# Expert jobs of 96 rows in place of 128 in a two-layer hybrid model kernel

## What is computed

```python
def swiglu(h, w1, w3, w2):
    return (jax.nn.silu(h @ w1) * (h @ w3)) @ w2

def moe_swiglu(h, w_router, w1, w3, w2):
    logits = (h @ w_router).astype(jnp.float32)
    top_v, top_i = lax.top_k(logits, TOP_K)            # TOP_K = 2
    gates = jax.nn.softmax(top_v, axis=-1)
    ...
    for e in range(N_EXPERTS):                          # 8
        out = out + combine[..., e:e + 1] * swiglu(h, w1[e], w3[e], w2[e])
```

## Time and profile before

| what | value |
|---|---|
| runs | 1646.36, 1650.67 and 1651.36 us, median 1650.67 |
| span of the profiled execution | 1645.5 us |
| PE busy | 1585.1 us, 96% of the span |
| DVE busy, ACT busy | 1283.7 us, 1041.8 us |
| expert part | from 672.4 us to 1634.4 us of the span |
| weights of the expert part | 336 loads of 1 MB |

### The profile page before, as it was taken

One profiled execution on the slowest core, in us unless ns is written; L12 is line 12 of the kernel. 1 busy time (PEld: TensorE's weight loads), 2 busy tenths in 40 slices (PEclk: granted clock), 3 DMA queues, 4 the chain that ended last, 5 costly groups with the idle time before them and its releaser, 6 DMA issues.

```text
span 1645.5 us, 27766 instructions
## 1 busy us (share of the span) xinstructions
PE 1585.1 (96%) x10290; PEld 1363.3 (83%) x10290; DVE 1283.7 (78%) x1252; ACT 1041.8 (63%) x1038; POOL 139.9 (9%) x152
## 2 busy tenths in 40 slices
PE   7999989999899999899999999999999999999997
PEld 7987789999898778788888888888888888888776
DVE  4885556555558656688889889889888888988997
ACT  4634454344354445577777777777777777777675
POOL 1062000000006200100000000000000000001720
PEclk9999999999999999999999999999999999999999
DMA  7429165542252105699999999999999999999992
GB/s 252 159 89 398 55 256 184 186 170 99 80 176 88 40 2 225 247 374 375 382 375 374 389 375 377 382 374 384 378 375 361 399 373 367 395 373 369 398 356 111
DMA packets 68272, 457.56 MB, mean 278 GB/s; under 512 B 7296, under 2 KB 8480, under 8 KB 16752
## 3 DMA queue, kind: packets, MB, share of 16 engines
q1 hardware_dynamic: 59984, 425.80, 67.1%
q0 software_dynamic: 8080, 30.84, 4.9%
q10 hardware_dynamic: 144, 0.05, 0.0%
HBM read 433.07 MB, written 23.59 MB: 278 GB/s over the span
## 4 chain that ended last, share of the span: by engine, by line
PE 54%; issue 3%; DVE 3%; ACT 2%; DVEq 0%; ACTq 0%
PE bank L417 33%; PE bank L442 17%; DVE wl L495 2%; PE bank L430 1%; ACT wh L491 1%; PE bank L738 1%; PE bank L1271 1%; DVE gl L586 0%; PE bank L814 0%; PE bank L1276 0%; PE bank L483 0%; DVE gate L577 0%; ACT wide L1770 0%; ACT oh L728 0%; DVE rstd L2026 0%
## 5 line engine op out<-in xcount | busy, mean ns | idle before, releaser
L495 DVE TENSOR_TENSOR wl<-ring,wh 128x2048 fp32r<-128x2048 f32 x369 | 854.0, 2318 | 157.7 <-ACT wh L491 154.4
L491 ACT ACTIVATE wh<-ring 128x2048 fp32r<-128x2048 f32 x369 | 706.6, 1917 | 99.5 <-PE bank L442 46.9
L417 PE MATMUL bank<-wh,xh 128*128 128x512 f32 x896 | 358.0, 400 | 3.6 <-DVE wl L495 3.0
L417 PE MATMUL bank<-wh,xl 128*128 128x512 f32 x896 | 350.3, 391 | 0.0
L417 PE MATMUL bank<-wl,xh 128*128 128x512 f32 x896 | 349.6, 390 | 0.0
L417 PEld LDWEIGHTS bank<-wh,xh 128*128 128x128 f32 x896 | 168.3, 188 | 36.7 <-DVE wl L495 3.7
L417 PEld LDWEIGHTS bank<-wh,xl 128*128 128x128 f32 x896 | 168.2, 188 | 35.5
L417 PEld LDWEIGHTS bank<-wl,xh 128*128 128x128 f32 x896 | 168.7, 188 | 32.2
L442 PE MATMUL bank<-wh,gh 128*128 128x512 f32 x448 | 175.4, 392 | 6.3 <-DVE gl L586 6.3
L442 PE MATMUL bank<-wh,gl 128*128 128x512 f32 x448 | 174.4, 389 | 0.0
L442 PE MATMUL bank<-wl,gh 128*128 128x512 f32 x448 | 174.3, 389 | 0.0
(11 more groups left out here) (336 smaller groups left out, 2434.2 us busy)
## 6 DMA issues: line engine op xcount, KB each, us to landing
ring<-in_moe_w SPq DMA_DIRECT2D x336, 1024.0 KB, 5.0
ring<-in_ffn_w SPq DMA_DIRECT2D x33, 1024.0 KB, 4.8
ring<-in_w_in SPq DMA_DIRECT2D x24, 1024.0 KB, 4.9
ring<-in_w_out SPq DMA_DIRECT2D x8, 1024.0 KB, 4.8
job_x<-xrow POOLq DMA_DIRECT2D x1, 8192.0 KB, 27.3
job_y<-xrow POOLq DMA_DIRECT2D x1, 8192.0 KB, 47.7
xrow<-job_x POOLq DMA_DIRECT2D x7, 512.0 KB, 9.3
job_y<-yj POOLq DMA_DIRECT2D x7, 512.0 KB, 4.4
```

Of the source, the lines that this page charges most:

```text
L417: ins = nc.tensor.matmul(up_bank(run, par, 0)[:], x[:, 0:C], w[b][:, k], **kw)
L491: nc.scalar.activation(wh[:, buf], flat_slot(slot), ACT.Copy).then_inc(sem("w_high"), 1)
L495: nc.vector.tensor_tensor(wl[:, buf], flat_slot(run.place(i)[0]), wh[:, buf].bitcast(F32), ALU.subtract).then_inc(sem("w_split"), 1)
```

## The change

`C` becomes 96. Every place where C and the number of partitions P were the same number is told apart: tiles that hold one row of a job in each partition use 96 partitions, matmuls whose stationary operand is the job's rows have 96 stationary columns, and matmuls and transposes whose output's free dimension is the rows have 96 columns. The buffers in DRAM have 16 x 96 rows. The comparison that counts an expert's jobs is made for b = 1 and b = 2 where it was made for b = 1. No instruction of a loop is added, removed or moved on any engine. The core of the diff:

```diff
-C = P
+C = 96
                             if run.moe:
-                                ins = nc.tensor.matmul(up_bank(run, par, 0)[:], x[:, 0:C], w[b][:, k], **kw)
+                                ins = nc.tensor.matmul(up_bank(run, par, 0)[0:C], x[:, 0:C], w[b][:, k], **kw)
                 for a in range(2):
-                    ins = nc.tensor.transpose(bank[TURNS][:, a * P:(a + 1) * P], gate[:, 0, a * P:(a + 1) * P], cst("id"))
+                    ins = nc.tensor.transpose(bank[TURNS][:, a * C:(a + 1) * C], gate[0:C, 0, a * P:(a + 1) * P],
+                                              cst("id")[0:C, 0:C])
                         if run.moe:
-                            ins = nc.tensor.matmul(bank[2 + o][:], g[:, a, 0:C], w[b][:, a, o * 512:(o + 1) * 512],
+                            ins = nc.tensor.matmul(bank[2 + o][0:C], g[:, a, 0:C], w[b][:, a, o * 512:(o + 1) * 512],
-                nc.scalar.activation(silu[:, item], up_bank(run, par, item)[:, 0:T], ACT.Silu, bias=cst("zero")
+                nc.scalar.activation(silu[0:C, item], up_bank(run, par, item)[0:C, 0:T], ACT.Silu, bias=cst("zero", C)
-                nc.vector.tensor_tensor(gate[:, item], up_bank(run, par, item)[:, T:2 * T], silu[:, item], ALU.mult
+                nc.vector.tensor_tensor(gate[0:C, item], up_bank(run, par, item)[0:C, T:2 * T], silu[0:C, item], ALU.mult
-                        turn(bank[5 + half][:, d * C:(d + 1) * C], xrow[:, k * P:(k + 1) * P],
-                             sig="gathered" if d == 3 else None)
+                        turn(bank[5 + half][:, d * C:(d + 1) * C], xrow[0:C, k * P:(k + 1) * P], C,
+                             "gathered" if d == 3 else None)
-                    nc.vector.tensor_tensor(xl[:, hv, 0:C], bank[5 + half][:].rearrange("p (k c) -> p k c", c=C),
+                    nc.vector.tensor_tensor(xl[:, hv, 0:C], bank[5 + half][:, 0:4 * C].rearrange("p (k c) -> p k c", c=C),
-                pool.dma_start(xrow[:], job_x[bass.ds(j * C, C), :]).then_inc(sem("x_loaded"), 16)
+                pool.dma_start(xrow[0:C], job_x[bass.ds(j * C, C), :]).then_inc(sem("x_loaded"), 16)
```

More of the change, by code:

```diff
@@ L792, in yrow, with placed @@
             return (xT, wide)[tt][:].rearrange("p (a b) t -> p a (b t)", a=2)[:, i]
-        def placed(tt=slice(0, TT)):
-            return gh[:, tt, C:2 * C]
+        def placed(tt):
+            return gh[0:C, tt, P:2 * P]
         def y_part(low, half):
-            return (xh, xl)[low][:, 4 * half:4 * half + 4, C:2 * C]
+            return (xh, xl)[low][0:C, 4 * half:4 * half + 4, P:2 * P]
         def acc_half(half):
-            return bank[2 + half][:].rearrange("p (k c) -> p k c", c=C)
+            return bank[2 + half][0:C].rearrange("p (k c) -> p k c", c=P)
         LAST_BANKS = ((5, 6), (0, 1))
@@ L881, in pe_moe @@
             for tt in range(TT):
-                turn(bank[7][:, tt * P:(tt + 1) * P], sel[:, tt], sig="place_turned" if tt else None)
+                turn(bank[7][0:C, tt * P:(tt + 1) * P], sel[:, tt], sig="place_turned" if tt else None)
             pe_down(pe, run, last, True)
@@ L904, in gathered @@
                     nc.scalar.activation(xh[:, 4 * half:4 * half + 4, 0:C],
-                                         bank[5 + half][:].rearrange("p (k c) -> p k c", c=C), ACT.Copy
+                                         bank[5 + half][:, 0:4 * C].rearrange("p (k c) -> p k c", c=C), ACT.Copy
                                          ).then_inc(sem("x_high"), 1)
@@ L911, in acc @@
                 for half in range(2):
-                    nc.scalar.copy(yj[:, half * 512:(half + 1) * 512], bank[2 + half][:]).then_inc(sem("acc_copied"), 1)
+                    nc.scalar.copy(yj[0:C, half * 512:(half + 1) * 512], bank[2 + half][0:C]).then_inc(sem("acc_copied"), 1)
             last = PAIRS_E - 1
@@ L935, in act_moe @@
             act.wait_ge(sem("place_turned"), 1)
-            nc.scalar.activation(placed(), bank[7][:, 0:T].rearrange("p (a c) -> p a c", c=C), ACT.Copy).then_inc(sem("last_high"), 1)
+            nc.scalar.activation(gh[0:C, :, P:2 * P], bank[7][0:C, 0:T].rearrange("p (a c) -> p a c", c=P), ACT.Copy).then_inc(sem("last_high"), 1)
             f(tiny[:], cst("zero"), ACT.Sqrt)
@@ L1003, in dve_moe @@
             for i in range(2):
-                settle(nc.vector.tensor_tensor(hit[:, i], cst("iota").unsqueeze(1).broadcast_to([P, TT, C]),
+                settle(nc.vector.tensor_tensor(hit[:, i], cst("iota")[:, 0:C].unsqueeze(1).broadcast_to([P, TT, C]),
                                                choice("slot")[:, i].unsqueeze(2).broadcast_to([P, TT, C]), ALU.is_equal))
@@ L1077, in load @@
             def load(j):
-                pool.dma_start(xrow[:], job_x[bass.ds(j * C, C), :]).then_inc(sem("x_loaded"), 16)
+                pool.dma_start(xrow[0:C], job_x[bass.ds(j * C, C), :]).then_inc(sem("x_loaded"), 16)
             def store(j):
                 pool.wait_ge(sem("acc_copied"), 2 * j + 2)
-                pool.dma_start(job_y[bass.ds(j * C, C), :], yj[:]).then_inc(sem("y_stored"), 16)
+                pool.dma_start(job_y[bass.ds(j * C, C), :], yj[0:C]).then_inc(sem("y_stored"), 16)
             pool.dma_start(fin, A["final_norm"].rearrange("(a d) -> a d", a=1).broadcast_to([P, D])
@@ L1253, in _ @@
                         pool.dma_start(rows_.rearrange("(j p) d -> p j d", p=C),
-                                       xrow[:].unsqueeze(1).broadcast_to([P, MAXJOBS, D])).then_inc(sem(sig), 16)
+                                       xrow[0:C].unsqueeze(1).broadcast_to([C, MAXJOBS, D])).then_inc(sem(sig), 16)
                 settle(nc.gpsimd.memset(xft[H:P, :, 0:H], 0.0))
```

## The result

The change took 1657.11 us, the median of 6 runs (1650.28 to 1658.58), against 1647.51 us, the median of 6 runs of the kernel before (the three known ahead and three more). The ratio is 1.0044 with a 95% interval of 1.0028 to 1.006: a little slower, clear of the noise, where 1644.4 us had been forecast. (The ratios here are not quotients of the medians. The profiled execution took 1650.28 us with a span of 1648.7, 3.2 us over the span of before.

The account below looks back on a forecast made before the run. PE's pace was taken to bound the expert part, most of the time. Transposes 4.8, hand-over 0.9 and start and end 0.6 summed to 6.3 us off 1650.67, giving 1644.4 us, range 1630 to 1652.

Parts of the forecast that it names:

- The 4032 large matmuls: Expert matmuls streaming 512 columns past the narrowed operand: starts stay 227 ns apart, loads hidden; 0 us, at most 13 less.
- Number of jobs: Router result: no expert has more than 78 rows, so eight jobs stay eight; a ninth would cost 119 us.
- Transposes: 4.8 us: Two PE transposes a pair move 96 columns instead of 128: 50 ns less in 12 pairs of each of 8 jobs.
- Hand-over: 0.9 us: DVE between jobs: two shorter `gl`, 67 ns less each, over 7 hand-overs.
- Start and end: 0.6 us: Shorter operations before job 0's first down projection and at the end, between 0 and 0.8 us less.
- Costed at nothing: Row loads, `yj` stores and zero fills become a quarter smaller but are covered, so 0 us.
- 1 (transposes keep their time): Transposes bound by the 128-column load or a fixed cost: 1.5 us gain remains, 1649.2 us, no change; chance 0.17.
- 2 (the 13 ns shrink: The rest in the large matmuls' 227 ns shrinks with width: 19 us less in total, 1631 us; chance 0.10.
- 3 (a drain at each switch of shape: Switching between 96 and 128 rows empties PE around the transposes: 32 us more, 1676 us; chance 0.08.
- 4: The router gives nine jobs instead of eight: 1763 us; chance 0.01.
- 5: Weight loads of the large matmuls are exposed after all: 26 ns each, 105 us less, 1540 us; chance 0.01.

Follow-up runs that it names:

- run 2: The kernel before with only the large matmuls' stationary operand narrowed to 96 columns; 1658.14 us, ratio 1.0061.
- run 5: The changed kernel itself measured again, unaltered, over 12 runs; 1653.44 us, ratio 1.002.
- run 1: The changed kernel with the large matmuls' stationary operand 128 columns wide again, columns 96 to 127 zeroed on DVE; 1650.66 us, ratio 1.002.
- run 11: The kernel before with the stationary weights of layer 0's dense up projection narrowed from 128 to 96 columns, 256 streamed; 1643.1 us, one run.
- run 12: The changed kernel with 128-wide stationary operands, zero fills from 128 partitions, and columns 96 to 127 zeroed at DVE's expert start, off the routing chain; 1643.70 us, ratio 0.9964.
- 8: The changed kernel with its two DRAM buffers at their old size of 2048 rows; 1656.36 us, ratio 1.0044.
- 10: The changed kernel with the zero fills of the 1536 rows made from 128 partitions; 1651.68 us, ratio 1.002.

## Why the prediction was wrong, by its own steps

**The 4032 large matmuls: "nothing". This is the step that failed.** I read 227 ns as 213 ns of stream and 13 ns of unknown nature, and let these 13 ns stay or shrink with the load, but never grow. At 96 columns they became 17: 4032 x 3.3 ns = 13 us by the arithmetic of the step. Of that 8.8 us reached the span in run 2. The matmuls right behind the transposes, a third of all, were at 229 ns already and lost only 1, which leaves some 10 us, and part of these lies beside DVE in the hand-overs and the last job. With the forecast -6.3 us for all other terms, 8.8 give +2.5, which is what the spans of before and of run 5 differ by. Two readings led there. "389 ns at both widths" are durations of fp32 matmuls, and it was the starts that moved, in fp32r. And the bounds came from one mechanism, a load that shows in part; no row of before had 96 stationary columns under a stream of 512, so a loss should have been an end of the range too.

**Number of jobs:** eight, right, and the page shows it by the 336 loads.

**Transposes: 4.8 us.** Right where they stand: 50 ns a pair, 245 ns each. In run 1, where nothing else in the pair changed, the twelve matmuls behind them took some 20 ns more (2.77 us against 2.75), so that a pair kept 0.03 to 0.035 us and a job 0.49 less instead of 0.73.

**Hand-over: 0.9 us.** Right: `gl` 351 ns, 0.14 us a job measured against 0.13.

**Start and end: 0.6 us.** Somewhat less came: from PE's work ahead of the routing to the first large matmul 9.38 us against 9.47, where 0.25 less was reckoned; from there to the first down projection 0.31 less against 0.27; at the end 0.04 against 0.15.

**Costed at nothing.** The transfers are covered, as I said: weights landing in 6.2 and in 7.1 us went with the same jobs of the change. The zero fills didn't get shorter but longer, 36.2 us, as did the row loads (11.7 us against 9.3 in the median), and stayed covered too. The clock I hadn't priced at all. It differs from run to run, and a thousandth of it is worth some 1.3 us: before had 0.9886 on average over 87 runs, the change 0.9860 over the 6 first runs and 0.9878 over 12 more. That is 2.3 of the some 4 us between the first ratio and the second. Set to the same clock of 0.988 by a line fitted to each set of runs, before took 1649.3 to 1650.2 us, the change 1653.1 to 1653.6: 3 to 4 us more.

**The rivals.** 1 (transposes keep their time): no, 0.17 us. 2 (the 13 ns shrink): the right place, with the wrong sign at 512 columns; at 256, in run 11, the sign is the right one. 3 (a drain at each switch of shape, 0.33 us a pair): no, the transposes with both their borders fit in 0.17 us. 4: no. 5: no, loads of 162 and 188 ns lie hidden at either pace. *TensorE: Matmul & The Clock Gate* of the Trainium skill, section Part 3 (The mechanism), says that a load overlaps running matmuls only when the row group differs. By that the narrow load would have saved 26 ns a matmul; run 2 lost 3.3. The section also names a background weight buffer as a second case of overlap, and the hidden loads don't speak against that one. The same page's section on weight-path perf modes gives fast weight load to exactly 128 columns outside fp32. The loss at five narrower widths looks like that, but the durations of the loads don't: 181 ns at 120 columns and 188 at 128 lie on the line of the narrower ones, and in run 11 the narrower operand wins.

**What it comes to.** The forecast for everything but the width was near: run 12 has jobs of 96 rows without the narrow operand (and with the two zeroing operations and fills from 128 partitions) and took 1643.7 us, where 1644.4 was forecast. Its span is 6.0 us under before's, where 6.3 was forecast. Inside it two misses cancel, which is luck: the six jobs in the middle gave 0.54 us each and not 0.73, the last one gave 1.55.

**Open.** Why 128 columns give the fastest pace at 512, and why 96 beat them at 256: the pace, the load and their order were seen, the mechanism wasn't. Nor is it shown why weights land later in kernels with jobs of 96 rows. Also open is whether the mean clock of the change is really lower than before's. It was so in all four sets with this pace (the result and runs 5, 8 and 10): 0.9873 over 42 runs against 0.9886, by 0.0005 to 0.0015 against the runs beside them in the last three. The fills, the buffers' places and job 0's gather were each tried, and none of them shows a cause.

## What to carry to other kernels

Give an unknown rest in an engine's pace both signs in the range, and measure the pace from start to start at the very shape and in the very place: the durations of another shape and type (389 ns at both widths) didn't show the 3 ns that 4032 matmuls made into 9 us, and the pace behind a pair of transposes was another one than elsewhere. When a tile gets smaller, shrink the operations whose streamed size falls, and try the stationary operand at full width separately: here the jobs of 96 rows gained only with 128 stationary columns. Keep even short extra operations off a chain on which PE waits, because the matmuls behind it may run at half clock.

## What the runs showed of the hardware

- With one load each, fp32r matmuls of 512 columns start 227 ns apart past 128 stationary columns, 230 past 64 or 96, about 231 past 112, and 233 past 80 or 120. Right behind two transposes they start 229 ns apart past 128 or 104 columns, and 230 to 232 past 96 or 32. At 256 columns they start 120 ns apart past 128 and 116 past 96.
- Loads of 80 to 128 stationary columns last 148 to 188 ns, some 0.83 ns a column, and are hidden at each of these paces: a load that shows would put starts at least 148 + 213 ns apart.
- PE's wait of 4.69 us in place of 4.17 stood ahead of 7 us at 1.2 GHz, in both profiles that had it; in the twelve others the wait was 4.17 to 4.19 and the same 32 matmuls took 3.81 to 3.84 us in place of 7.07.
- The zero fill of `job_x`, with that of `job_y` issued behind it, takes 36.2 us for 6 MB from 96 partitions and 22.0 from 128; 8 MB from 128 took 27.3.
